# Hybrid GLA / Gated-DeltaNet trunk on one core: the second mixer's chunk inverse spread over other windows, and three edits where its scan begins

## What is computed

```python
def gdn_mixer(h, w_in, conv_w, a_log, dt_bias, head_norm, w_out):
    proj = h @ w_in                                   # q, k, v, z, beta, a
    qkv = silu(causal_depthwise_conv(qkv, conv_w))    # 4 taps
    q = l2_norm(q) * DK ** -0.5;  k = l2_norm(k)
    beta = sigmoid(beta_logit)
    log_a = -exp(a_log) * softplus(a_logit + dt_bias)
    # per chunk of 64 tokens (the 16 meta tokens are a chunk of their own):
    g = cumsum(log_a)
    decay = exp(g_i - g_j) for j <= i
    m = strict_lower((k * beta) @ k.T * decay)
    u, w = solve(I + m, [v * beta, k * beta * exp(g)])
    # from chunk to chunk, with state s:
    v_new = u - w @ s
    o = (q * exp(g)) @ s + (q @ k.T * decay) @ v_new
    s = s * exp(g_last) + (k * exp(g_last - g)).T @ v_new
    return (rms_norm(o) * head_norm * silu(z)) @ w_out
```

## Time and profile before

| | us |
|---|---|
| median of three runs | 1534.98 (1532.82 to 1536.03) |
| the profiled execution, its own time | 1536.11 |
| its span, first to last instruction | 1534.3 |
| TensorE busy | 1444.4 (94%) |
| VectorE busy | 789.5 (51%) |
| ScalarE busy | 429.0 (28%) |
| GpSimd busy | 381.4 (25%) |
| mean granted TensorE clock | 0.983 |

### The profile page before, as it was taken

How to read it: one execution, slowest core, us unless ns; L and a number is a source line. 1 busy time by engine, 2 the same in 40 slices (tenths; PEclk the granted TensorE clock), 3 DMA queues, 4 the chain that set the end, 5 groups by cost and what they waited for, 6 DMA issues and landing times.

```text
span 1534.3 us, 21430 instructions
## 1 busy us (share of the span) xinstructions
PE 1444.4 (94%) x8490; PEld 1211.2 (79%) x8490; DVE 789.5 (51%) x1017; ACT 429.0 (28%) x914; POOL 381.4 (25%) x303
## 2 busy tenths in 40 slices
PE   6999999975999999999999989999998999999997
PEld 4777779973788779999999988978886667777775
DVE  4213612222444437654556799989933654444432
ACT  4322832103222214333332422212222531111111
POOL 3212123415111112221221221222343342222200
PEclk9999999997999999999999999999999999999998
DMA  5520214526645314345345232235359794555530
GB/s 186 176 83 28 98 55 125 160 105 228 191 166 171 121 55 115 92 113 137 101 118 197 70 84 72 70 97 179 109 189 240 199 253 135 147 148 155 155 83 28
DMA packets 213853, 200.81 MB, mean 131 GB/s; under 512 B 62840, under 2 KB 177032, under 8 KB 213504
## 3 DMA queue, kind: packets, MB, share of 16 engines
q1 hardware_dynamic: 207168, 187.99, 41.1%
q10 hardware_dynamic: 6592, 11.54, 2.8%
HBM read 132.39 MB, written 67.09 MB: 130 GB/s over the span
## 4 chain that ended last, share of the span: by engine, by line
PE 42%; DVE 13%; issue 3%; ACT 3%; DMA 2%; ACTq 0%; POOLq 0%; DVEq 0%; SPq 0%; POOL 0%
PE banks L2564 11%; PE banks L1898 11%; PE banks L1832 9%; DVE gdn L2102 6%; PE banks L2644 2%; PE banks L2612 2%; PE banks L2614 2%; DVE gdn L2099 1%; PE banks L1726 1%; DMA gdn<-in_gdn_w_out 1%; PE banks L1750 1%; PE banks L2630 1%; PE banks L2623 1%; DVE gdn L2107 1%; ACT gdn L1966 1%
## 5 line engine op out<-in xcount | busy, mean ns | idle before, releaser
L1832 PE MATMUL banks<-hn_hi,gdn 128*128 128x352 f32 x1488 | 303.6, 329 | 0.0
L1832 PEld LDWEIGHTS banks<-hn_hi,gdn 128*128 128x128 f32 x1488 | 243.9, 190 | 4.1 <-issue 2.7
L2077 POOL TENSOR_TENSOR gdn<-gdn,gdn 128x1024 fp32r<-128x1024 f32 x31 | 99.8, 3220 | 316.8 <-ACT gdn L1934 316.8
L2102 DVE SCALAR_TENSOR_TENSOR gdn<-gdn,conv_taps,gdn 128x1040 f32<-128x1040 f32 x96 | 162.2, 1689 | 3.4
L1898 PE MATMUL banks<-gdn,hn_hi 128*128 128x512 f32 x512 | 161.8, 396 | 0.4 <-DVE gdn L2109 0.4
L1832 PE MATMUL banks<-hn_lo,gdn 128*128 128x352 f32 x744 | 159.1, 322 | 0.0
L1832 PEld LDWEIGHTS banks<-hn_lo,gdn 128*128 128x128 f32 x744 | 126.7, 189 | 0.0
L1898 PEld LDWEIGHTS banks<-gdn,hn_hi 128*128 128x128 f32 x512 | 95.5, 188 | 26.3 <-issue 2.6
L750 PE MATMUL ai_p<-ai_whi,hn_hi 128*128 128x512 f32 x264 | 106.0, 402 | 5.5 <-DVE ai_wlo L575 2.5
L750 PE MATMUL ai_p<-ai_wlo,hn_hi 128*128 128x512 f32 x264 | 104.8, 397 | 0.0
L750 PE MATMUL ai_p<-ai_whi,hn_lo 128*128 128x512 f32 x264 | 104.3, 395 | 0.0
(11 more groups left out here) (287 smaller groups left out, 2477.1 us busy)
## 6 DMA issues: line engine op xcount, KB each, us to landing
gdn<-in_gdn_w_in SPq DMA_DIRECT2D x32, 512.0 KB, 4.1
ai_st<-in_gla_w_in SPq DMA_DIRECT2D x32, 256.0 KB, 4.7
gdn_kq<-gdn SPq DMA_DIRECT2D x16, 512.0 KB, 3.9
gdn_v<-gdn SPq DMA_DIRECT2D x16, 512.0 KB, 3.5
gdn<-in_gdn_w_in SPq DMA_DIRECT2D x32, 256.0 KB, 4.6
gdn<-gdn_kq SPq DMA_DIRECT2D x16, 512.0 KB, 3.7
gdn<-gdn_ek SPq DMA_DIRECT2D x16, 512.0 KB, 5.3
gdn<-gdn_v SPq DMA_DIRECT2D x32, 256.0 KB, 6.7
```

The source lines that it names most:

```text
L1832: last = pe.matmul(a[:, b, 0:m], w[n % 2][:, kt, :], x[:, kt, PAD + s:PAD + s + m], start=(kt == 0 and e == 0), stop=(kt == KT - 1 and e = ...
L2077: pool.tensor_tensor(lo[n % 2][:, :, :], st[n % 2][:, :, :], hi[n % 2][:, :, :].bitcast(F32), ALU.subtract).then_inc(S("ni_wlo"), 1)
L2102: dve.scalar_tensor_tensor(cv[:, :], xs[:, tap:tap + L], T.cw[:, tap, t:t + 1], cv[:, :], ALU.mult, ALU.add).then_inc(S("ni_conv"), 1)
```

## The change

- VectorE: `distances` is cut in two, its first half a window earlier (18) and the rest where it was (19). `exponents` keeps its small steps in window 21, and its last part becomes `differences`, in window 22.
- ScalarE: `exps` moves from window 22 to window 23.
- VectorE: portions of the inverse are taken from window 24 on and not 23, until 2800 is used up and not 4200. What isn't taken there runs behind v.
- SP: `load_ek(1)` goes behind the wait for the large store and `load_ua(0)`.
- TensorE: `meta` takes six of its 26 filling products ahead of its first waits, and 10 in place of 16 at its end.

No instruction is added or taken away; the operations and their shapes are the same.

```diff
-                if n == v_tile(5):
+                if n == v_tile(6):
                     exps()
...
-            def distances():
+            HALVES = ((slice(0, 32), slice(0, C)), (slice(32, C), slice(32, C)))
+
+            def distances(n):
...
-                for n, (r, c) in enumerate(((slice(0, 32), slice(0, C)), (slice(32, C), slice(32, C)))):
-                    form = [P, 32, c.stop - c.start]
-                    dve.tensor_tensor(dm_rows[:, r, c], bc(gc[:, r, :], form), bc(gr[:, :, c], form), ALU.subtract)\
-                       .then_inc(S("ni_dd"), 1)
+                r, c = HALVES[n]
+                form = [P, 32, c.stop - c.start]
+                dve.tensor_tensor(dm_rows[:, r, c], bc(gc[:, r, :], form), bc(gr[:, :, c], form), ALU.subtract)\
+                   .then_inc(S("ni_dd"), 1)
+                if n == 0:
+                    return
...
                 dve.tensor_tensor(m_kd[:, :], m_kd[:, :], m_ln[:, :], ALU.subtract).then_inc(S("ni_expo"), 1)
+
+            def differences():
                 dve.wait_ge(S("ni_dd"), 3)
...
-                if n == v_tile(2):
-                    distances()
+                if n in (v_tile(1), v_tile(2)):
+                    distances(n - v_tile(1))
...
+                if n == v_tile(5):
+                    differences()
                 if n == v_tile(8):
                     scale_k()
-                left = 4200 if n >= v_tile(6) else 0
+                left = 2800 if n >= v_tile(7) else 0
                 while left > 0:
                     left -= next(inverse)
...
             load_kt(1)
-            load_ek(1)
             sp.wait_ge(S("ni_ua_out"), 16)
             load_ua(0)
+            load_ek(1)
...
             def meta(fill):
+                fill(6)
                 pe.wait_ge(S("ni_zev"), F.tiles + 2)
...
-                fill(16)
+                fill(10)
```

## The result

The changed kernel takes 1543.85 us (median of 4, 1542.73 to 1546.51) against 1535.14 us (1532.82 to 1536.03) for the kernel before: ratio 1.0062, 95% interval [1.0044, 1.0079], **8.7 us slower**. The range ended at 1542.8, and the forecast of 1537.8 was 6 us short. The profiled execution took 1542.73 us, 6.6 more than that of before; what follows explains those 6.6.

The account below looks back on a forecast made before the run. TensorE and VectorE were taken as nearly full beside v, with VectorE having 24.9 us spare behind. Meta products +2.5, six fills -1.4 and low clock +1.7 gave +2.8 us on the median 1534.98: 1537.8, range 1532.5 to 1542.8.

Parts of the forecast that it names:

- What bounds the kernel, and v's windows: v's tiles: TensorE and VectorE both nearly full; moving inverse work behind v lets z begin 9.2 us earlier, at 993.1.
- the 1.8 us of tile 32: Stall beside v: window 31, with 6.7 us of inverse work and a late start, leaves 1.8 us more.
- Rival (c): v's tiles: a full stall from window 23's late copy cuts v's gain to 5 us; 1542, within the 0.43.
- I take 0.6 us, nearer the lower end: Rest of the inverse behind v: GpSimd's splits of z's weights hold VectorE for 0.6 us, bounds 0 and 5.
- I take 13.4: From the inverse's end to the landing of the meta step's loads, queued behind the large store: 13.4 us, bounds 12.5 and 14.5.
- TensorE stands for some 12.6 us: Before the meta products: TensorE waits some 12.6 us in one piece for the meta step's loads.
- The clock: Behind TensorE's long wait: the clock at 0.50 for 3.4 us more costs +1.7 us, bounds 1.0 and 3.4.
- SP's order worth 0, six fills 1.4: Scan's start: SP's new load order gains 0; six products put first save 1.4 us behind the wait.
- All behind: Scan after the meta step: all later loads keep their distance of 10 us to the first chunk, cost 0.
- Rival (b): VectorE's tail: GpSimd's splits hold it 4 us more, or the clock stays low for two stretches; 1542, chance 0.43.

Follow-up runs that it names:

- The kernel with a budget for each window: Changed kernel with 48 filling products ahead of the meta step's waits and a separate budget for each of windows 24 to 32 in place of 2800: 1524.48 us.
- the kernel with the meta inverse first: Changed kernel with the meta tokens' small inverse at the start, not the end, of what runs behind v: 1542.32 us.
- 48 fills ahead: Changed kernel with 48 filling products in place of 6 ahead of the meta step's waits, total unchanged: 1535.65 us.
- 4200 and 48 fills: Changed kernel with 48 filling products ahead of the meta step and 4200 in place of 2800 in every window from 24 on: 1535.34 us.
- part 1 alone: Kernel before with only the preparation spread (distances, exponents and exponentials a window apart), portions of 4200 from v_tile(6) kept: 1536.02 us, ratio 1.0017.

## Why the prediction failed, step by step

- **What bounds the kernel, and v's windows**: right. Rest of the inverse from 1008.53 (forecast 1008.6; this execution had begun 1.0 late, so v gained 1.1 more than forecast), stalls of 0.8, 0.7 and 4.3 us where 0.6, 0.9 and 4.3 were given; the 1.8 us of tile 32 did not come. Rival (c) is out.
- **"I take 0.6 us, nearer the lower end"**, the holding by GpSimd: this term failed. It was 6.4, beyond my upper bound of 5. The bound counted the splits by their usual distance of 5.6 us over the added 24 us, and only against the added instructions. It missed that z's last five splits come 1.7 us apart, and that what is moved is not only the added work but the tail behind it, small instructions that had run in the open. That a reduction isn't held was right here and beside the point, as the end of the tail has none. The kernel with a budget for each window shows the same from the other side: its tail ends before the burst, and 6 us of holds are gone. The Trainium skill (SBUF — State Buffer, "Who interferes with whom") states an exclusive lock; 0.21 us instructions that last until the end of GpSimd's 1.3 us agree.
- **"I take 13.4"**, store and loads: 14.85, past my upper bound of 14.5, in spite of the z stores being over. Six kernels give 14.6 to 14.9. The store took 12.3 us, about as before (12.1); the landing behind the last issue was longer (8.2 us for the 32 KB loads, 7.2 in the earlier trace rows). Why it was, no run shows.
- **"TensorE stands for some 12.6 us"**: right in kind and place, 19.7 in size, by the two terms above.
- **The clock**, +1.7: 2.1 in this trace, within its bounds, though a shorter wait cost 7.2 in another kernel, as the last section shows.
- **SP's order worth 0, six fills 1.4**: the first is right by the traces; the second fits the 1.4 us measured, which is no more than the noise.
- **"All behind", 0**: -3.8 in the profiled executions, which hid part of the miss. Without it the sum would have been +10.4.
- **Rival (b)** was the case that came. I had given it 4 us; its holding alone was 5.8 over the forecast. The range ended too soon because both bounds of VectorE's tail were taken from places that the change moves away from.

## What to carry to other kernels

When work is moved behind a stage, walk the other engine's instructions through the times at which the tail will now run, not the times at which it ran: here each of the six instructions of a burst held one instruction of VectorE, however small that one's own work. Before unloading an engine that has spare time later, add what hangs behind its last instruction (here 14.9 us of store and loads) to see how much spare time it truly has. A yield budget can be cut per window, by what that window can take (1524.48 us, where one budget for all windows gave 1535.65 and 1535.34), and a wait that is left should first be given the independent work that stands behind it.

## What the hardware showed

- **The price of a low clock did not follow the length of the wait before it.** Summed over the stretches behind the meta products, full clock less granted clock times length is 2.3 us behind the 19.7 us wait of the changed kernel (0.5 x 3.4 + 0.17 x 3.6), and 7.2 behind the 15.0 us wait of the kernel with the meta inverse first (0.50, 0.50, 0.50, 0.59 over 15.2 us). With 48 fills ahead it is 5.7 behind a wait of 9.8 us. Behind no wait but the 1.5 us one, with 4200 and 48 fills, it is 3.4, of which these two stretches hold 3.2:

```profile
1168.00:1172.00 4.00, 4.00 (x17) 2.99 (x18) 1.73 (x5) 0.60 (x1) 0.00 (x0) 0.50 1.16 299
1172.00:1176.00 4.00, 4.00 (x16) 2.82 (x17) 1.11 (x4) 0.00 (x0) 0.00 (x0) 0.69 0.46 137
```

  What decides it was not tried. The Trainium skill (TensorE: Matmul & The Clock Gate, "What's actually happening") has the low level as the default that activity lifts. The rows agree: the clock fell to 0.50 within the 19.7 us wait and was full again from 1168 on, behind it. They add that TensorE, busy 4.00 of 4.00 us by the profile, stood at 1.2 GHz for over 11 us (1161 to 1172 in the kernel with the meta inverse first).
- **Four GpSimd splits that meet VectorE's long instructions took 8.60 us for 5.2 us of work**, where they took 6.5 with their gaps in the changed kernel: either engine holds the other, and swapping the order of VectorE's work moved the hold from one to the other.
- **Executions with equal instructions in the first chunk differ by 1.6 us** in its period: 21.7 us in part 1 alone and 23.3 in before, with a wait of 2.6 us in either; the clock fell behind it in before (0.66, 0.91) and stayed full in the other.
